# Interleaving the key-index product with the transposes of x at the head of a two-block transformer kernel

## What is computed

```python
hn = rmsnorm(h, norm_mix_g[i])
proj = h @ w_in                      # h is hn here; w_in has D_MODEL rows
qi = proj[..., o3:o4].reshape(b, length, IDX_HEADS, IDX_DIM).astype(jnp.float32)
ki = layernorm(proj[..., o4:o5], idx_k_g, idx_k_b).astype(jnp.float32)
wi = proj[..., o5:].astype(jnp.float32) * (IDX_HEADS ** -0.5 * IDX_DIM ** -0.5)
```

## Time and profile before

| what | value |
|---|---|
| median of 3 runs | 1993.64 us (1992.79 to 1993.82) |
| the profiled execution | 1993.12 us, of which the span is 1991.3 us |
| TensorE busy | 1849.9 us, 93% of the span |
| ScalarE busy | 749.3 us, 38% |
| VectorE busy | 883.9 us, 44% |
| GpSimd busy | 795.5 us, 40% |
| mean granted TensorE clock | 0.969 of full speed |
| weights and x read from memory | 156.90 MB |

### The profile page before, as it was taken

The page is one execution under the profiler, slowest core; times in us unless marked ns, Lnnn a source line. Parts: engine busy times, 40 slices in busy tenths (PEclk is TensorE's granted clock), DMA queues, the critical chain, the costliest instruction groups (busy, mean ns, idle before and its releaser), DMA issues.

```text
span 1991.3 us, 20374 instructions
## 1 busy us (share of the span) xinstructions
PE 1849.9 (93%) x8018; PEld 1446.8 (73%) x8018; DVE 883.9 (44%) x1396; ACT 749.3 (38%) x1175; POOL 795.5 (40%) x358
## 2 busy tenths in 40 slices
PE   7999999999999977749999999999899899999987
PEld 6687778888888754227888888877777688667665
DVE  3693532200201799973210111187757631335463
ACT  4423444312422432425331232344444332444442
POOL 3343123444444445824444444333344443333211
PEclk9999999999999988879999999999999899999999
DMA  5232112233233211002333333332232233232101
GB/s 179 67 99 75 43 55 95 92 104 101 86 106 95 74 57 60 11 0 79 101 95 96 95 103 99 96 106 75 74 95 85 72 99 95 77 89 74 48 27 42
DMA packets 100094, 160.31 MB, mean 81 GB/s; under 512 B 7296, under 2 KB 30208, under 8 KB 100000
## 3 DMA queue, kind: packets, MB, share of 16 engines
q1 hardware_dynamic: 100000, 159.02, 25.9%
HBM read 156.90 MB, written 2.10 MB: 80 GB/s over the span
## 4 chain that ended last, share of the span: by engine, by line
PE 42%; DVE 7%; ACT 3%; issue 2%; POOL 1%; DMA 0%; SPq 0%; POOLq 0%; DVEq 0%; ACTq 0%
PE bank L580 13%; PE bank L581 12%; PE bank L582 12%; PE bank L873 2%; POOL w_lo L2299 1%; DVE gla_state L2215 1%; DVE rg_t L2013 1%; PE bank L1027 1%; DVE rg_t L2002 1%; PE bank L1010 1%; ACT w_hi L1125 1%; DMA gate_w<-in_rg_gate_w 0%; DVE rg_i L2009 0%; DVE rg_sq L2001 0%; DVE rg_y L2016 0%
## 5 line engine op out<-in xcount | busy, mean ns | idle before, releaser
L2299 POOL TENSOR_TENSOR w_lo<-w_raw,w_hi 128x1024 fp32r<-128x1024 f32 (+1 forms) x286 | 694.9, 2436 | 1116.7 <-ACT w_hi L1125 1116.6
L580 PE MATMUL bank<-x_hi,w_hi 128*128 128x512 f32 (+1 forms) x1264 | 512.9, 406 | 38.0 <-DVE conv_lin L1685 19.6
L1125 ACT ACTIVATE w_hi<-w_raw 128x1024 fp32r<-128x1024 f32 (+1 forms) x286 | 299.6, 1054 | 557.2 <-PE bank L582 551.0
L581 PE MATMUL bank<-x_lo,w_hi 128*128 128x512 f32 (+1 forms) x1264 | 498.7, 395 | 0.0
L582 PE MATMUL bank<-x_hi,w_lo 128*128 128x512 f32 (+1 forms) x1264 | 498.4, 394 | 0.0
L580 PEld LDWEIGHTS bank<-x_hi,w_hi 128*128 128x128 f32 (+1 forms) x1264 | 240.9, 191 | 100.7 <-issue 33.4
L581 PEld LDWEIGHTS bank<-x_lo,w_hi 128*128 128x128 f32 (+1 forms) x1264 | 240.8, 190 | 55.7 <-issue 5.6
L582 PEld LDWEIGHTS bank<-x_hi,w_lo 128*128 128x128 f32 (+1 forms) x1264 | 240.4, 190 | 52.8
L580 PE MATMUL bank<-w_hi,f_hi 128*128 128x512 f32 x512 | 200.0, 391 | 0.0
L582 PE MATMUL bank<-w_hi,f_lo 128*128 128x512 f32 x512 | 199.3, 389 | 0.0
L581 PE MATMUL bank<-w_lo,f_hi 128*128 128x512 f32 x512 | 199.2, 389 | 0.0
(11 more groups left out here) (273 smaller groups left out, 2176.8 us busy)
## 6 DMA issues: line engine op xcount, KB each, us to landing
w_raw<-in_mlp_w SPq DMA_DIRECT2D x128, 512.0 KB, 3.7
w_raw<-in_even_w_in SPq DMA_DIRECT2D x48, 512.0 KB, 3.8
w_raw<-in_dsa_w_in SPq DMA_DIRECT2D x28, 512.0 KB, 3.5
w_raw<-in_odd_w_in SPq DMA_DIRECT2D x24, 512.0 KB, 3.7
w_raw<-in_conv_w_pw SPq DMA_DIRECT2D x32, 256.0 KB, 3.0
w_raw<-in_even_w_out SPq DMA_DIRECT2D x16, 512.0 KB, 4.1
w_raw<-in_dsa_w_out SPq DMA_DIRECT2D x8, 512.0 KB, 3.8
w_raw<-in_conv_w_pw SPq DMA_DIRECT2D x8, 512.0 KB, 3.8
```

The source lines that it names most:

```text
L580: e.matmul(o, sh, mh, start=first, stop=False)
L581: e.matmul(o, sh, ml, start=False, stop=False)
L1125: e.activation(hi, src, ACT.Copy).then_inc(*w_hi.up(u))
L2299: e.tensor_tensor(lo, src, hi.bitcast(F32), ALU.subtract).then_inc(*w_lo.up(u))
```

## The change

On TensorE alone, the generator of the index rows is made before the loop of the transposes. In the loop, from tile 2 on, each pass asks it for its next value, and what is left of it is run out behind the loop. Every instruction is kept; no wait is taken away or added by hand.

```diff
+            def x0(k, t=0):
+                return x_lo.at(0, k)
+
+            rows = by_features("idx", X, x0)
             for k in range(KD):
                 for t in range(T):
                     w.wait_ge(*con_in.last())
...
                     m = e.transpose(bank[k][:, t * P:(t + 1) * P], H[:, t, k * P:(k + 1) * P], ident)
                 m.then_inc(*turned.up(0, k))
                 free[k] = x_lo.at(0, k)
-
-            def x0(k, t=0):
-                return x_lo.at(0, k)
-
-            for k in by_features("idx", X, x0):
+                if k >= 2:
+
+                    next(rows)
+            for k in rows:
                 pass
             free[0] = index_act.at("narrow")
```

## The result

The changed kernel took 1996.98 us in the median of 17 runs (1994.11 to 1997.99), against 1992.79 us for the kernel before in 17 runs of the same session (1990.80 to 1997.60). The ratio is 1.0019, with a 95% interval from 1.0012 to 1.0027: 2.4 to 5.4 us slower, most likely 3.8. That is inside the range (1993.3 to 1997.8), of the sign that was forecast, and its centre lies just under the +0.2% line. The median of 1996.98 lies near the upper end of the range, which was set by a clock falling in the new hole.

A forecast was written before the change was run, and what follows sets the result against it. TensorE was taken to bound the kernel. The late `w_lo` of unit 1 adds 2.0 us (2.8 late less 0.9 slack, and 0.1) to the median of 1993.64, giving 1995.6 us; range 1993.3 to 1997.8.

The forecast's parts named there:

- the sign that was forecast: Whole kernel: slower, by +2.0 us against the profiled execution.
- the new hole: TensorE before the first qi matmul: a new idle stretch of about 1.6 us, 19.8 to 21.4.
- What bounds the kernel: TensorE, busy 93% of the span, with no gap from 9.65 us until the qi product; moved rows fill no hole.
- With no switch cost, +1.7: Lower bound of the head's +2.0 us delay, if TensorE's switches between transposes and index rows cost nothing.
- four returns: TensorE's added switches from index rows back to transposes, charged 0.08 us each, 0.3 in all.
- the term: First qi matmul, delayed by unit 1's late `w_lo`: +2.0 us (2.8 late less 0.9 slack, and 0.1).
- The chain tile 7, `x_hi`, unit 1, `w_lo`, qi product: Head: tile 7's `x_hi` 2.8 us late delays unit 1's rounding and `w_lo`; first qi matmul moves from 19.53 to 21.5.
- The wait of 3.10 before `make_row` neither shrinks nor grows: TensorE's wait for VectorE's diagonals stays near 3.1 us, since VectorE's chain moves by the same 2.0 us.
- The first rival: TensorE's clock falls to 1.2 GHz in the idle stretch before the qi product: 1.7 us more, 1997.3 us; chance 0.15.
- The clock rising earlier: Rival at the head: index rows mixed in from 11.4 us bring 2.4 GHz sooner, 1993.8 us; chance 0.03.

The follow-up runs named there:

- unit 1 early: Changed kernel with ScalarE's rounding of weight unit 1 put between x tiles 5 and 6; ratio 1.0004 to the kernel before, median 1993.08 us.
- `make_row` late: Kernel before with make_row behind qi row 6, the keys' turn behind row 5: 1987.43 us; with weight unit 1 also rounded early: 1987.91 us.

## Why the prediction was right, and what it missed

- **What bounds the kernel.** Right. TensorE had no gap to fill from 9.65 us on, and the moved rows won nothing.
- **"With no switch cost, +1.7".** The chosen value charged 0.08 us for each of four returns. With unit 1 early the head is 8.12 against 8.18, so the returns cost nothing (four transposes and a row take 16.96 - 15.83 = 1.13 us interleaved, and 0.43 + 0.70 apart). ScalarE's `x_hi` of tile 7 is late by 2.4 us at an equal clock (17.60 - 9.08 - 3.03 against 14.45 - 9.65 - 1.70), not 2.8, and the term is 1.5 to 1.6, just under the lower bound.
- **The chain tile 7, `x_hi`, unit 1, `w_lo`, qi product.** Right, and shown from three sides: by taking it away, by making it without the change, and by the number of rows.
- **"The wait of 3.10 before `make_row` neither shrinks nor grows".** This is the step that failed. It followed who waits for whom, and left out that VectorE and GpSimd hold each other up: GpSimd's late units reach into VectorE's keys, +0.45 us in both profiles of the change.
- **The clock.** The first rival put the fall into the new hole. It did not fall there (the granted clock is 1.00 in all stretches from 17 to 30 us), so the case that set the upper end of the range did not come. That the range holds the median of 1996.98 is in part luck: it lies above what the sum below explains. It is the old hole, 0.45 longer, behind which the slow stretch was in some profiles 1.1 us dearer.
- **The clock rising earlier.** It had a chance of 0.03 and is not settled. The slow stretch behind quarter 1 lasted 3.4, 4.3, 4.7, 5.1 and 5.5 us in the five profiles with TensorE's old order at the head, and 2.7, 2.7, 2.8, 3.3, 3.4, 3.9 and 6.1 in the seven with interleaving; the 6.1 is the first profile of the change. If that is more than chance, the interleaving gave back some 0.5 us, and more of its cost is unexplained.

The sum as the runs have it: 1.5 for the head, 0.6 up to `make_row` and about 0.5 for the clock behind it make 2.6 us. Both intervals for the change hold it, 2.4 to 5.4 and 1.0 to 4.8; their centres, 3.8 and 2.8, lie above. What is left over, 1.2 us at the one centre and 0.2 at the other, stays open. Laid against the first profile of the kernel before, matmul by matmul, every profile keeps a constant distance from 95 us to 700 us. From there to the end it changes, by something between -3.1 and +0.8 us, and by +0.8 in the second profile of the kernel before; so single profiles can't place the rest.

## What to carry to other kernels

When work is moved forward on the engine that bounds a kernel, look at what is moved back by it, and at the in-order queue of the engine that it feeds: here four rows of 0.7 us stood in front of the last transposes, and a weight rounding that had nothing to do with either came 2.4 us late. A chain of waits is not the whole price of a delay: two engines that share ports may slide over each other. And the largest idle stretch of the bounding engine is the first place to look; one product moved two rows back there gave 5.2 us, more than the change cost.

## What the runs showed of the hardware

- TensorE went over to its fast spacing behind transposes alone in three of the five profiles with that order, 3.4, 4.7 and 4.3 us behind the landing of quarter 1. In the other two (`make_row` late, 5.5 and 5.1 us) all 24 transposes kept the slow spacing, and it rose as the first index row began. Over all twelve profiles, it took between 2.7 and 6.1 us of unbroken work, and moves the head by up to 1.7 us between runs.
- A VectorE operation of 0.3 us on 64 columns, from SBUF to SBUF, is held for the whole of a GpSimd operation of 2.4 us that starts just before it (2.35 us); a batch-norm statistic on the same 64 columns under such an operation still took 0.23.
- An idle stretch of 1.4 to 1.75 us left TensorE's clock at 2.4 GHz in each of the five profiles that had one at the head; the one of 3.1 to 4.4 us before `make_row` took it to 1.2 GHz in all eight that had it. In one profile of twelve it fell at 86 us with no idle stretch from 20 us on, behind eight matmuls 0.43 us apart.
